# Host-turned x in six parts, and every third low half of layer 1 on GpSimd, in a four-layer fp32 forward pass

## The chip, the cores and the metric

The kernel runs on one NeuronCore of a Trainium2 chip. The metric is the device time of one execution in microseconds (us). Engines are called by the names of the profile: PE is the matmul engine (TensorE; PEld its weight loads), DVE is VectorE, ACT is ScalarE, POOL is GpSimd, SP is the engine that issues most DMAs.

## What is computed

x is 256 tokens by 2048 features. Four layers follow each other, each of the same outer form, and a last norm:

```python
proj = rmsnorm(x, norm_g) @ w_in          # 2048 -> 6160 .. 9224 columns
y = mixing(proj)                          # attention, mLSTM, RG-LRU, gated delta, ...
x = x + y @ w_out                         # 2048 -> 2048
...
def gated_delta_chunkwise(q, k, v, beta, g):      # layer 1
    a_mat = where(strict, (kbeta @ k^T) * gam, 0)
    t_inv = triangular_solve(eye + a_mat, eye)
    u, w = t_inv @ (v * beta), t_inv @ (kbeta * exp(decay))
    ...
```

Layer 0 is a chunked attention beside an mLSTM, layer 1 an RG-LRU beside the gated delta rule above, layers 2 and 3 are softmax attentions with rotary embedding. Everything is float32.

## The kernel before

**Products.** All big products are done in three passes of the fp32r type: a weight tile is split into a high half (its value rounded to fp32r) and a low half (weight minus high half), and so is the activation. Then high x high, high x low and low x high are added in PSUM. The weights stream from HBM in transfers of 1 MB into three buffers RAW. Each holds two **pieces** of 128 x 1024 values. For a piece ACT writes the high half (`split` of ACT, L981, WH<-RAW), DVE the low half (`split` of DVE, L1295, WL<-RAW,WH), in four buffers each, and PE does 24 products of 256 columns (L687 to L689) or 12 of 512 (L680 to L682). There are 626 pieces, numbered through the whole program. `load` on SP waits for the low halves of the transfer three before, which frees its buffer.

**Order.** Nothing is scheduled at run time but by semaphores: every engine runs through the pieces p = 0, 1, 2, ... in the same loop and does for each: the splits that fall due (`splits_of`, those of piece p+3 as a rule), the steps that the table `plan` puts half a place ahead of p, the `products` of p (PE), the `evacuate` of the job whose last piece p is (`ENDS`), and the steps that `plan` puts behind p. `put(slot, step, item, wants)` writes that table by hand, `begin_plan` for the start and `plan1` for layer 1. A step has the same place on every engine that takes part. If an engine waits within a step, all its later steps and splits wait behind it. Small products go through four PSUM banks PM in turn (`bank`): a step waits until the reader of the step four banks back is done.

**Start (layer 0).** x comes as rows of tokens. PE turns it to features by tokens with 32 transposes (`xt`, L703), ACT makes the high half of x times the norm's gain (L1048, XH<-PM), DVE the low half (L1349, XL). ACT also squares x for the norm (`squares`, L1056), DVE sums (`rms_a`), PE spreads the row scale (`rms_b`, L712). SP issues in this order: ident (64 KB of the constants), x part 0 of 4 (512 KB), both halves of weight transfer 0, x part 1, weight transfer 1, x parts 2 and 3, the rest of the constants (704 KB), row parameters (204 KB), weight transfer 2. POOL loads two bias tiles at once.

**Layer 1.** It starts at piece b1 = 177. Below, "piece 1.k" is piece b1+k. For two halves of four heads each it runs: `conv` (ACT scale L1142, DVE taps L1525, ACT silu L1148), `norm_sq` on POOL, `norm_sum`, `turn_v` (PE transposes L857 of v, ACT copies L1179), `diag` on POOL, `delta_a`, `delta_k`, `delta_q` (PE L864 to L877, ACT exponentials L1185 to L1187, DVE L1591 to L1611), `tri` in ten parts (a chain of small DVE operations, L1618 to L1643, and ACT copies L1194, L1199), `level_x` and `level_y` (PE L891, L905, L908, ACT L1209, DVE L1650, L1654), `solve1` to `solve4`, `onorm`, `gate_delta`, and `ty` (turned back for the product with w_out). Beside them run the eight blocks of the RG-LRU (`gate_lru`, `decay_lru`, `root_lru`, `scan`). POOL multiplies, from SBUF to SBUF: the evacuated conv inputs (L1794), the gates (L1800, L1874, L1881), and it clears and masks for `tri` (L1862 to L1864).

Of the kernel before, what the change touches and what calls it, by code (L numbers as in the profile page):

```python
# [20 lines left out]
LOOK = 3  # L21

# [118 lines left out]
def program(nc, I, out):  # L141
    ctx = ExitStack()
    with ctx:
# [167 lines left out]
        ENDS = {p: j for j, p in LAST.items()}  # L311
# [44 lines left out]

        def begin_plan():
# [65 lines left out]
        def plan1():  # L423
# [88 lines left out]

        def around(p):

            return ([x for s in (p - 0.5,) for x in plan.get(s, ())], plan.get(p, ()))


        s_c0, s_c1, s_mask, s_lam, s_tab, s_gw, s_fin, s_first, s_out = (
            sem(n) for n in ("s_c0", "s_c1", "s_mask", "s_lam", "s_tab", "s_gw", "s_fin", "s_first", "s_out"))
        s_x = [sem(f"s_x{i}") for i in range(4)]  # L520
        s_raw = [sem(f"s_raw{i}") for i in range(NRAW)]
        s_bias = [sem(f"s_bias{i}") for i in range(2)]
        s_hi, s_lo, s_mm, s_evA, s_evD = (sem(n) for n in ("s_hi", "s_lo", "s_mm", "s_evA", "s_evD"))
# [62 lines left out]
        n_id, n_cos, n_dil = COFF["ones"][0], COFF["cos"][0], COFF["dilated"][0]  # L586
# [5 lines left out]
        def sync(e):  # L592
# [8 lines left out]
            def load(n):  # L601
                j, k0, nk = raws[n]
                dst = RAW[n % NRAW][:, 0:nk * jobs[j].n].rearrange("p (k n) -> p k n", k=nk)
                if n >= NRAW:
                    e.wait_ge(s_lo, last_of_raw[n - NRAW] + 1)
                e.dma_start(dst, weights(n)).then_inc(s_raw[n % NRAW], 16)

            e.dma_start(C[:, 0:n_id], I["const"][:, 0:n_id]).then_inc(s_c0, 16)
            load_x(0)
# [3 lines left out]
            load_x(1)  # L613
            load(1)
            load_x(2)
            load_x(3)
            e.dma_start(C[:, n_id:n_dil], I["const"][:, n_id:n_dil]).then_inc(s_c1, 16)
            e.dma_start(RB[:, :], I["row"].partition_broadcast(128)).then_inc(s_c1, 16)
            load(2)
            again = pieces[F(2, "zs", 0)][0] + NRAW  # L620
            for n in range(NRAW, len(raws)):
                if n == again:
                    e.wait_ge(s_evD, at_D(2, "k1", 1))
                    e.dma_start(C[:, n_cos:n_dil], I["const"][:, n_cos:n_dil]).then_inc(s_tab, 16)
                load(n)
            o3 = out.rearrange("(t p) c -> p t c", p=128)
# [10 lines left out]
        def tensor(e):  # L637
# [8 lines left out]
            def products(p):  # L646
# [6 lines left out]
                e.wait_ge(s_lo, p + 1)  # L653
# [37 lines left out]

            def xt(i, b):
                layer, q = divmod(i, 8)
                if layer == 0:
                    e.wait_ge(s_x[q // 2], 16)
                    if q == 0:
                        e.wait_ge(s_c0, 32)
                else:
                    e.wait_ge(s_evD, at_D(layer - 1, "out", q // 2))
# [253 lines left out]
            steps = {"xt": xt, "rms_b": rms_b, "gates1": gates1, "gates2": gates2, "decay": decay, "mscores": mscores, "qkT": qkT,  # L953
# [19 lines left out]
        def scalar(e):  # L973
            e.dma_start(VC[:, :], I["vec"]).then_inc(s_c0, 16)
# [65 lines left out]

            def xt(i, b):
                layer, q = divmod(i, 8)
                if i == 0:
                    e.wait_ge(s_c0, 32)
                e.wait_ge(s_xt, i + 1)
# [216 lines left out]
            steps = {"xt": xt, "squares": squares, "root": root, "rms_a": rms_a, "gates1": gates1, "decay": decay, "pT": pT,  # L1262
# [11 lines left out]
            for p in range(NP):  # L1274
                before, after = around(p)
                for q in splits_of(p):
                    split(q)
                go(before)
                if p in ENDS:
                    evacuate(ENDS[p], p)  # L1280
# [10 lines left out]
        def vector(e):  # L1291
# [51 lines left out]

            def xt(i, b):
# [7 lines left out]
            def rms_a(layer, _):  # L1352
# [3 lines left out]
                e.reciprocal(rstd, rstd).then_inc(s_rstd)  # L1356
                if layer < 4:
# [377 lines left out]
            steps = {"xt": xt, "rms_a": rms_a, "rms_b": rms_b, "gates1": gates1, "gates2": gates2, "decay_row": decay_row,  # L1735
# [14 lines left out]
            for p in range(NP):  # L1750
                before, after = around(p)
                for q in splits_of(p):
                    split(q)
                go(before)
                if p in ENDS:
                    evacuate(ENDS[p], p)
# [14 lines left out]
        def gpsimd(e):  # L1771
            def evacuate(j, p):
# [41 lines left out]
            def norm_qk(_, b):  # L1814
                load_bias(0)
# [92 lines left out]
            for p in range(NP):  # L1908
                before, after = around(p)
                go(before)  # L1910
                if p in ENDS:
                    evacuate(ENDS[p], p)
# [6 lines left out]
def arrange(a):  # L1919
# [7 lines left out]
    m["x"] = _np.ascontiguousarray(a["x"][0])  # L1927
    t, c = _np.arange(128)[:, None], _np.arange(32)[None, :]
# [41 lines left out]
```

## Time and profile before

| | |
|---|---|
| median of 3 runs | 1970.77 us (1970.48 to 1971.33) |
| the profiled execution's own time | 1970.41 us |
| its span | 1968.6 us |
| PE busy | 1932.7 us (98%) |
| DVE busy | 1166.8 us (59%) |
| ACT busy | 1005.2 us (51%) |
| POOL busy | 172.6 us (9%) |
| HBM read | 334.47 MB, 171 GB/s over the span |

Busy is the time in which an engine executes instructions. PE's 98% leave 36 us in which it has no instruction. The chain that ended last is PE for 94% of the span. The granted clock of PE is full (2.4 GHz) in all but a few short stretches.

### The profile page before, as it was taken

Reading aid. Unit: us, or ns where it says so; the run is one execution under the profiler, and the core shown is the slowest. Engines: PE = TensorE matmul, PEld = TensorE weight load, DVE = VectorE, ACT = ScalarE, POOL = GpSimd, SP = SyncE. Lnnn points to the kernel's source line nnn. Section 1 sums busy time; section 2 is a strip of 40 time slices with the busy share of each in tenths; the row PEclk is TensorE's granted clock in tenths of the full one; section 3 lists DMA queues with packets and bytes.
Section 4 is the critical chain, followed back from the end, with each engine's and each line's share of the span. In section 5 each row is a group of like instructions: output and inputs, shape, how many; then the busy total and the mean of one; then the engine's idle time right before and its main releaser. Section 6 shows DMA issues by size and latency. Waiting matters only on the chain.

```text
span 1968.6 us, 28920 instructions
## 1 busy us (share of the span) xinstructions
PE 1932.7 (98%) x11932; PEld 1736.6 (88%) x11932; DVE 1166.8 (59%) x1635; ACT 1005.2 (51%) x1547; POOL 172.6 (9%) x162
## 2 busy tenths in 40 slices
PE   8999999999999999989999999999999999999997
PEld 7988888888899999889899899888889989988886
DVE  5445554555556776877566567655556656654554
ACT  5344445664556645755553344556554344445643
POOL 0000000110003211301001001000000101100110
PEclk9999999999999999999999999999999999999999
DMA  7555455555554443434555654554555554455553
GB/s 266 172 192 171 160 187 193 162 170 192 173 172 130 135 143 130 150 129 168 175 182 191 194 174 157 183 191 157 172 190 173 188 190 158 158 190 166 170 194 128
DMA packets 172851, 338.44 MB, mean 172 GB/s; under 512 B 9536, under 2 KB 9920, under 8 KB 172592
## 3 DMA queue, kind: packets, MB, share of 16 engines
q1 hardware_dynamic: 171632, 332.83, 51.4%
q0 software_dynamic: 944, 3.61, 0.6%
q8 instruction: 95, 1.56, 0.3%
q14 instruction: 36, 0.29, 0.0%
q10 hardware_dynamic: 144, 0.16, 0.0%
HBM read 334.47 MB, written 2.10 MB: 171 GB/s over the span
## 4 chain that ended last, share of the span: by engine, by line
PE 94%; DVE 3%; ACT 1%; issue 1%; DMA 0%; SPq 0%; DVEq 0%; ACTq 0%
PE ACC L680 17%; PE ACC L682 17%; PE ACC L681 17%; PE ACC L687 11%; PE ACC L688 11%; PE ACC L689 11%; DVE WL L1295 1%; DVE S L1525 1%; PE PM L770 1%; PE PM L703 1%; PE PM L785 1%; ACT WH L981 1%; PE PM L823 1%; PE PM L891 1%; PE PM L807 1%
## 5 line engine op out<-in xcount | busy, mean ns | idle before, releaser
L1295 DVE TENSOR_TENSOR WL<-RAW,WH 128x1024 fp32r<-128x1024 f32 x624 | 782.9, 1268 | 623.6 <-ACT WH L981 622.1
L981 ACT ACTIVATE WH<-RAW 128x1024 fp32r<-128x1024 f32 x626 | 652.2, 1054 | 544.8 <-PE ACC L682 303.3
L687 PE MATMUL ACC<-XH,WH 128*128 128x256 f32 x1920 | 554.2, 289 | 3.9 <-DVE WL L1295 3.7
L688 PE MATMUL ACC<-XL,WH 128*128 128x256 f32 x1920 | 545.9, 284 | 0.0
L689 PE MATMUL ACC<-XH,WL 128*128 128x256 f32 x1920 | 545.9, 284 | 0.0
L680 PE MATMUL ACC<-WH,XH 128*128 128x512 f32 x1024 | 406.5, 397 | 0.0
L682 PE MATMUL ACC<-WH,XL 128*128 128x512 f32 x1024 | 399.0, 390 | 0.0
L681 PE MATMUL ACC<-WL,XH 128*128 128x512 f32 x1024 | 398.7, 389 | 0.0
L687 PEld LDWEIGHTS ACC<-XH,WH 128*128 128x128 f32 x1920 | 371.5, 194 | 6.2 <-DVE WL L1295 4.7
L688 PEld LDWEIGHTS ACC<-XL,WH 128*128 128x128 f32 x1920 | 371.5, 193 | 0.9
L689 PEld LDWEIGHTS ACC<-XH,WL 128*128 128x128 f32 x1920 | 371.1, 193 | 0.0
L682 PEld LDWEIGHTS ACC<-WH,XL 128*128 128x128 f32 x1024 | 192.2, 188 | 40.6
L681 PEld LDWEIGHTS ACC<-WL,XH 128*128 128x128 f32 x1024 | 192.4, 188 | 39.0
L680 PEld LDWEIGHTS ACC<-WH,XH 128*128 128x128 f32 x1024 | 192.3, 188 | 38.8
L680 PE MATMUL ACC<-WH,YHB 128*128 128x512 f32 x256 | 100.8, 394 | 0.0
L680 PE MATMUL ACC<-WH,YHA 128*128 128x512 f32 x256 | 100.2, 391 | 0.0
L682 PE MATMUL ACC<-WH,YLB 128*128 128x512 f32 x256 | 99.8, 390 | 0.0
L682 PE MATMUL ACC<-WH,YLA 128*128 128x512 f32 x256 | 99.7, 389 | 0.0
L681 PE MATMUL ACC<-WL,YHB 128*128 128x512 f32 x256 | 99.6, 389 | 0.0
L681 PE MATMUL ACC<-WL,YHA 128*128 128x512 f32 x256 | 99.6, 389 | 0.0
L1806 POOL TENSOR_TENSOR S<-S 128x512 f32<-128x512 f32 x32 | 53.8, 1681 | 505.3 <-DVE S L1342 505.3
L682 PEld LDWEIGHTS ACC<-WH,YLB 128*128 128x128 f32 x256 | 48.0, 188 | 10.1
(328 smaller groups left out, 1646.2 us busy)
## 6 DMA issues: line engine op xcount, KB each, us to landing
RAW<-in_ev_w_in SPq DMA_DIRECT2D x71, 1024.0 KB, 4.9
RAW<-in_w_in_ab SPq DMA_DIRECT2D x64, 1024.0 KB, 5.2
RAW<-in_w_in_c SPq DMA_DIRECT2D x64, 1024.0 KB, 5.2
RAW<-in_od_w_in SPq DMA_DIRECT2D x48, 1024.0 KB, 5.0
RAW<-in_ev_w_out SPq DMA_DIRECT2D x16, 1024.0 KB, 4.9
RAW<-in_od_w_out SPq DMA_DIRECT2D x16, 1024.0 KB, 4.9
RAW<-in_w_out_ab SPq DMA_DIRECT2D x16, 1024.0 KB, 4.9
RAW<-in_w_out_c SPq DMA_DIRECT2D x16, 1024.0 KB, 4.9
```

The costliest lines, as they stand in the source:

```text
L680: e.matmul(o, th, hi[:, kk, :], start=f, stop=False)
L681: e.matmul(o, th, lo[:, kk, :], start=False, stop=False)
L682: m = e.matmul(o, tl, hi[:, kk, :], start=False, stop=l)
L687: e.matmul(o, wh, xh, start=f and g % 2 == 0, stop=False, skip_group_check=True)
L688: e.matmul(o, wh, xl, start=False, stop=False, skip_group_check=True)
L689: m = e.matmul(o, wl, xh, start=False, stop=l, skip_group_check=True)
L703: m = e.transpose(o[:, 256 * kk + 128 * t:256 * kk + 128 * t + 128], X3[:, t, 256 * q + 128 * kk:256 * q + 128 * kk + 128], ident)
L770: e.matmul(o[:, 128:384], qT[:, 128:256], kT, start=True, stop=True).then_inc(s_sc)
L785: m = e.transpose(o[:, c:c + 128], src[:, c:c + 128], ident)
L981: e.activation(hi, src, ACT.Copy).then_inc(s_hi)
L1295: e.tensor_tensor(lo, src, hi.bitcast(F32), ALU.subtract).then_inc(s_lo)
L1806: e.tensor_tensor(dst, dst, two(S6[:, 512 * i:512 * i + 512]), ALU.add).then_inc(s_rot)
```

## The change

**Start.** The host also hands over xT, x turned to features by tokens. SP loads it in six parts into Y, which is free then; ACT and DVE make XH and XL from there (`x0`), ahead of the split of the same features' weights. The transposes of layer 0 are gone. x itself, which the squares and the residual need, and the constants are loaded behind weight transfers 3 to 8. The squares stand at pieces 8 to 11 instead of 0 to 3, `rms_a` at 12, `rms_b` at 13.5, and the evacuation of job 0 seven pieces later. Ahead of piece 0 DVE clears 512 columns, PE does five products with them, and ACT one copy. The bias tiles wait until the row scale is there.

**Low halves.** 20 of the low halves of layer 1 (`BY_G`: pieces 1.35, 38, 41, 44, 52, 55, 58, 61, 64, 67, 70, 78, 81, 84, 87, 90, 93, 96, 99 and 102) are made by POOL. They count on a semaphore of their own, and PE and SP wait for whichever engine made the piece's low half (`low_of`).

**Later steps.** `turn_v` moves from 1.28 and 1.29 to 1.31 and 1.33 in half 0, and from 1.52 and 1.53 to 1.57 and 1.59 in half 1; the gates of half 0 by 3 to 4 places; levels, solves and gates of half 1 by 2.

```diff
+WARM = 5
...
-        ENDS = {p: j for j, p in LAST.items()}
+        ENDS = {p: (j,) for j, p in LAST.items()}
+        ENDS[LAST[0] + 7] = ENDS.pop(LAST[0])
...
+        X_PARTS = ((0, 2), (2, 2), (4, 2), (6, 2), (8, 4), (12, 4))
...
         def begin_plan():
-            for q in range(8):
-                put((-1, -0.5, 0.5, 2.5)[q // 2], "xt", q, 1)
+            put(-1, "warm")
             for b in range(4):
-                put((-0.5, 0.5, 2.5, 4)[b], "squares", b)
-            put(5, "rms_a", 0)
-            put(6.5, "rms_b", 0, 1)
+                put(8 + b, "squares", b)
+            put(12, "rms_a", 0)
+            put(13.5, "rms_b", 0, 1)
...
-            for half, at in ((0, (19, 22, 28, 29)), (1, (44, 48, 52, 53))):
+            for half, at in ((0, (19, 22, 31, 33)), (1, (44, 48, 57, 59))):
...
-                     (56, 58, 60, 61, 62), (82, 83, 85)),
-                    (1, (62, 63), (64, 66, 68, 69, 70), tuple(range(71, 81)), (81, 82, 84, 85, 86, 87), (89, 91, 93, 95, 96),
-                     (98, 99, 101))):
+                     (56, 58, 60, 61, 62), (85, 87, 89)),
+                    (1, (62, 63), (64, 66, 68, 69, 70), tuple(range(71, 81)), (83, 84, 86, 87, 88, 89), (91, 93, 95, 97, 98),
+                     (100, 101, 103))):
...
+        BY_G = [FIRST[J_OF[1, "qd", 0]] + i for i in (35, 38, 41, 44, 52, 55, 58, 61, 64, 67, 70, 78, 81, 84, 87, 90, 93, 96, 99, 102)]
+
+        def low_of(p):
+
+            g = sum(q <= p for q in BY_G)
+            return (s_loG, g) if p in BY_G else (s_lo, p + 1 - g)
...
+            load_xT(0)
             first = RAW[0][:, :].rearrange("p (k n) -> p k n", k=4)
             e.dma_start(first[:, 0:2, :], weights(0)[:, 0:2, :]).then_inc(s_first, 16)
             e.dma_start(first[:, 2:4, :], weights(0)[:, 2:4, :]).then_inc(s_raw[0], 16)
-            load_x(1)
+            load_xT(1)
             load(1)
-            load_x(2)
-            load_x(3)
-            e.dma_start(C[:, n_id:n_dil], I["const"][:, n_id:n_dil]).then_inc(s_c1, 16)
-            e.dma_start(RB[:, :], I["row"].partition_broadcast(128)).then_inc(s_c1, 16)
+            load_xT(2)
+            load_xT(3)
             load(2)
+            load_xT(4)
+            load_xT(5)
...
+            def warm(_, b):
+
+                e.wait_ge(s_warm, 1)
+                for _ in range(WARM):
+                    e.matmul(PM[0][:, :], S5[:, 1024:1152], S5[:, 1024:1536], start=True, stop=True)
...
+            def x0(q):
+                if q == 0:
+                    e.wait_ge(s_vec, 16)
+                for i, (k, n) in enumerate(X_PARTS):
+                    if k == 2 * q:
+                        e.wait_ge(s_xT[i], 16)
+                for n in (2 * q, 2 * q + 1):
+                    e.activation(XH3[:, n, :], Y[:, 256 * n:256 * n + 256], ACT.Copy, scale=gains[0][:, n:n + 1]).then_inc(s_xh)
...
         def gpsimd(e):
+            def split(p):
+                src, hi, lo = split_parts(p)
+                e.wait_ge(s_hi, p + 1)
+                e.tensor_tensor(lo, src, hi.bitcast(F32), ALU.subtract).then_inc(s_loG)
```

**How it moves instructions.** At the start of ACT's program (L1048 makes XH from PSUM, L981 a high half, L1056 squares) stands before:

```order
L1048 ACTIVATE XH<-PM,VC 128x256 x4
L981 ACTIVATE WH<-RAW 128x1024 x2
L1048 ACTIVATE XH<-PM,VC 128x256 x4
L1056 ACTIVATE SC,SM<-X 128x512 x2
L981 ACTIVATE WH<-RAW 128x1024 x3
```

and with the change (L1077 makes XH from Y, L1006 a high half):

```order
L1068 ACT_TABLE_LOAD
L1068 ACTIVATE SM<-S 128x1
L1077 ACTIVATE XH<-Y,VC 128x256 x2
L1006 ACTIVATE WH<-RAW 128x1024
L1077 ACTIVATE XH<-Y,VC 128x256 x2
```

The first high half stands behind two XH instead of four, and no square stands ahead of the third.

On ACT around pieces 1.28 to 1.31 (L1179 copies turned v, L1185 to L1187 are `delta_a`, L981 high halves) stands before:

```order
L1148 ACTIVATE S<-S 128x256 x2
L981 ACTIVATE WH<-RAW 128x1024
L1179 ACTIVATE S<-PM,SM 128x128 x4
L1185 ACT_TABLE_LOAD
L1185 ACTIVATE SC<-PM,SM 128x128
```

and with the change (the same three are L1215, L1221 to L1223 and L1006):

```order
L1184 ACTIVATE S<-S 128x256 x2
L1006 ACTIVATE WH<-RAW 128x1024
L1221 ACT_TABLE_LOAD
L1221 ACTIVATE SC<-PM,SM 128x128
L1222 ACTIVATE SC<-SC,SM 128x128
L1223 ACTIVATE SC<-SC,SM 128x128
L1006 ACTIVATE WH<-RAW 128x1024 x2
```

The copies of v are gone from between the silu of the conv and the exponentials of the second head.

On POOL from the second `diag` to the evacuation of job kd 1 stands before (L1794 multiplies conv inputs, L1862 to L1864 belong to `tri`):

```order
L1794 TENSOR_TENSOR S<-S,C 128x512 x2
L1862 MEMSET SC 128x1024
L1863 MEMSET SC 128x1024
L1864 TENSOR_TENSOR S<-SC,C 128x1024
L1794 TENSOR_TENSOR S<-S,C 128x512 x2
```

and with the change (L1825 is a low half, L1849 the multiply, L1918 to L1920 `tri`):

```order
L1825 TENSOR_TENSOR WL<-RAW,WH 128x1024
L1849 TENSOR_TENSOR S<-S,C 128x512 x2
L1825 TENSOR_TENSOR WL<-RAW,WH 128x1024
L1918 MEMSET SC 128x1024
L1919 MEMSET SC 128x1024
L1920 TENSOR_TENSOR S<-SC,C 128x1024
L1825 TENSOR_TENSOR WL<-RAW,WH 128x1024
L1849 TENSOR_TENSOR S<-S,C 128x512 x2
L1825 TENSOR_TENSOR WL<-RAW,WH 128x1024
```

The low halves of pieces 1.35, 1.38, 1.41 and 1.44 stand each ahead of the POOL work of the same place.

## Rows read from the trace of the kernel before

**Rows 1.** The page: busy us, share and instructions of each engine.
```profile
PE 1932.7 (98%) x11932; PEld 1736.6 (88%) x11932; DVE 1166.8 (59%) x1635; ACT 1005.2 (51%) x1547; POOL 172.6 (9%) x162
```

**Rows 2.** Waits of PE: waiting line, releaser, us in total, times, longest us.
```profile
PE PM L703 <- DMA X<-in_x: 8.8, 2, 6.1
PE PM L891 <- issue: 5.1, 1, 5.1
PE PM L864 <- ACT S L1179: 4.3, 1, 4.3
PE ACC L687 <- DVE WL L1295: 3.7, 3, 1.9
PE PM L905 <- DVE YLB L1513: 1.3, 1, 1.3
PE PM L905 <- ACT S L1179: 0.7, 1, 0.7
```

**Rows 3.** Timeline, 0 to 17 us: start, us, engine, line, operation, count [idle before].
```profile
6.13 1.97 PE L703 MATMUL PM<-C,X 128*128 128x128 f32 x8 [6.13 <-DMA X<-in_x]
...
10.07 2.02 ACT L981 ACTIVATE WH<-RAW 128x1024 fp32r<-128x1024 f32 x2
...
11.18 2.36 DVE L1295 TENSOR_TENSOR WL<-RAW,WH 128x1024 fp32r<-128x1024 f32 x2
...
12.46 0.58 PE L687 MATMUL ACC<-XH,WH 128*128 128x256 f32 x1
...
13.27 0.41 PE L687 MATMUL ACC<-XH,WH 128*128 128x256 f32 x1
...
15.09 0.28 PE L687 MATMUL ACC<-XH,WH 128*128 128x256 f32 x1
...
16.17 1.03 PE L703 MATMUL PM<-C,X 128*128 128x128 f32 x8
```

**Rows 4.** DMAs issued at 1.19, 1.66 and 8.61 us: size, us to landing.
```profile
X<-in_x SPq DMA_DIRECT2D x1, 512.0 KB, 4.9
RAW<-in_ev_w_in SPq DMA_DIRECT2D x1, 512.0 KB, 6.3
...
RAW<-in_ev_w_in SPq DMA_DIRECT2D x1, 1024.0 KB, 12.9
```

**Rows 5.** ACT's timeline ahead of piece 1.29.
```profile
640.11 0.81 ACT L1148 ACTIVATE S<-S 128x256 f32<-128x256 f32 x2 [1.16 <-DVE S L1525]
...
641.77 1.12 ACT L1179 ACTIVATE S<-PM,SM 128x128 f32<-128x128 f32 x4
```

**Rows 6.** Stretches: length, busy (count) of PE, PEld, DVE, ACT, POOL, granted clock, DMA.
```profile
643.00:645.00 2.00, 2.00 (x9) 1.82 (x8) 1.94 (x8) 1.22 (x2) 0.00 (x0) 0.50 0.03 8
...
848.00:854.00 6.00, 5.62 (x27) 5.65 (x28) 3.45 (x7) 5.76 (x10) 0.71 (x1) 0.52 0.00 1
```

**Rows 7.** Timeline of POOL and DVE where both read SBUF.
```profile
625.28 2.56 POOL L1794 TENSOR_TENSOR S<-S,C 128x512 f32<-128x512 f32 x2 [9.77 <-ACT S L1026]
...
626.61 2.31 DVE L1295 TENSOR_TENSOR WL<-RAW,WH 128x1024 fp32r<-128x1024 f32 x1 [2.70 <-ACT WH L981]
...
812.80 2.35 POOL L1864 TENSOR_TENSOR S<-SC,C 128x1024 f32<-128x1024 f32 x1
...
818.60 2.54 POOL L1800 TENSOR_TENSOR S<-S,RB 128x512 f32<-128x512 f32 x2 [1.81 <-ACT S L1032]
...
818.80 1.11 DVE L1630 TENSOR_TENSOR SC<-SC 128x16 f32<-128x16 f32 x1
819.94 1.22 DVE L1632 TENSOR_TENSOR SC<-SC 128x16 f32<-128x16 f32 x1
```

**Rows 8.** DVE's low half of piece 1.45.
```profile
697.11 1.22 DVE L1295 TENSOR_TENSOR WL<-RAW,WH 128x1024 fp32r<-128x1024 f32 x1 [1.43 <-ACT WH L981]
```

**Rows 9.** ACT's last copy of `tri`, half 1, and its high half of piece 1.84.
```profile
846.57 1.71 ACT L1199 ACTIVATE SC<-SC 32x256 f32<-32x256 f32 x4
...
850.84 1.04 ACT L981 ACTIVATE WH<-RAW 128x1024 fp32r<-128x1024 f32 x1
```

More of the change, by code:

```diff
@@ L585, in program @@
         x_rows = I["x"].rearrange("(t p) c -> p t c", p=128)
-        n_id, n_cos, n_dil = COFF["ones"][0], COFF["cos"][0], COFF["dilated"][0]
+        n_cos, n_dil = COFF["cos"][0], COFF["dilated"][0]
         block = ctx.enter_context(nc.Block())
@@ L604, in load, with load_xT @@
                 if n >= NRAW:
-                    e.wait_ge(s_lo, last_of_raw[n - NRAW] + 1)
+                    for p in range(last_of_raw[n - NRAW - 1] + 1 if n > NRAW else 0, last_of_raw[n - NRAW] + 1):
+                        e.wait_ge(*low_of(p))
                 e.dma_start(dst, weights(n)).then_inc(s_raw[n % NRAW], 16)
-            e.dma_start(C[:, 0:n_id], I["const"][:, 0:n_id]).then_inc(s_c0, 16)
-            load_x(0)
+            def load_xT(i):
+                e.dma_start(Y[:, part_of_x(i)], I["xT"][:, part_of_x(i)]).then_inc(s_xT[i], 16)
+            load_xT(0)
             first = RAW[0][:, :].rearrange("p (k n) -> p k n", k=4)
@@ L625, in sync @@
                 load(n)
+                if n < 7:
+                    load_x(n - 3)
+                if n == 7:
+                    e.dma_start(C[:, 0:n_dil], I["const"][:, 0:n_dil]).then_inc(s_con, 16)
+                if n == 8:
+                    e.dma_start(RB[:, :], I["row"].partition_broadcast(128)).then_inc(s_con, 16)
             o3 = out.rearrange("(t p) c -> p t c", p=128)
@@ L690, in products @@
                 m.then_inc(s_mm)
+            def warm(_, b):
+                e.wait_ge(s_warm, 1)
+                for _ in range(WARM):
+                    e.matmul(PM[0][:, :], S5[:, 1024:1152], S5[:, 1024:1536], start=True, stop=True)
             def xt(i, b):
                 layer, q = divmod(i, 8)
[L694 to L699, printed above, removed]
+                e.wait_ge(s_evD, at_D(layer - 1, "out", q // 2))
                 o = bank(b)
@@ L1039, in evacuate, with warm @@
                                      accum_out=ssq[:, 4 * t + J.b:4 * t + J.b + 1]).then_inc(s_sq)
+            def warm(_, b):
+                e.wait_ge(s_warm, 1)
+                e.activation(unused, S5[:, 1024:1025], ACT.Copy)
+            def x0(q):
[6 more added lines that the diff above has]
+                    e.activation(XH3[:, n, :], Y[:, 256 * n:256 * n + 256], ACT.Copy, scale=gains[0][:, n:n + 1]).then_inc(s_xh)
             def xt(i, b):
                 layer, q = divmod(i, 8)
[L1043 to L1045 removed]
+                e.wait_ge(s_xt, i - 7)
                 for kk in range(2):
@@ L1260, in subln @@
                     e.activation(ss, ss, ACT.Sqrt, bias=vec("eps"), scale=1.0 / 256).then_inc(s_sln)
-            steps = {"xt": xt, "squares": squares, "root": root, "rms_a": rms_a, "gates1": gates1, "decay": decay, "pT": pT,
+            steps = {"warm": warm, "xt": xt, "squares": squares, "root": root, "rms_a": rms_a, "gates1": gates1, "decay": decay, "pT": pT,
                      "norm_qk": norm_qk, "qkT": qkT, "scores": scores, "mix1": mix1, "pv": pv, "ty": ty, "conv": conv, "decays1": decays1,
@@ L1276, in scalar @@
                 for q in splits_of(p):
+                    if q < 8:
+                        x0(q)
                     split(q)
                 go(before)
-                if p in ENDS:
-                    evacuate(ENDS[p], p)
+                for j in ENDS.get(p, ()):
+                    evacuate(j, LAST[j])
                 go(after)
@@ L1342, in evacuate, with warm, x0 @@
                             e.tensor_tensor(t2[x], ps[y], sin[y], ALU.mult).then_inc(s_evD)
+            def warm(_, b):
+                e.memset(S5[:, 1024:1536], 0.0).then_inc(s_warm)
+            def x0(q):
+                e.wait_ge(s_xh, 2 * q + 2)
+                for n in (2 * q, 2 * q + 1):
+                    e.scalar_tensor_tensor(XL3[:, n, :], Y[:, 256 * n:256 * n + 256], gains[0][:, n:n + 1],
+                                           XH3[:, n, :].bitcast(F32), ALU.mult, ALU.subtract).then_inc(s_xl)
             def xt(i, b):
@@ L1356, in rms_a @@
                 e.reciprocal(rstd, rstd).then_inc(s_rstd)
+                if layer == 0:
+                    e.wait_ge(s_con, 32)
                 if layer < 4:
@@ L1733, in subln @@
                         e.scalar_tensor_tensor(y, y, ss[:, t, h:h + 1], row("subln"), ALU.mult, ALU.mult).then_inc(s_sub)
-            steps = {"xt": xt, "rms_a": rms_a, "rms_b": rms_b, "gates1": gates1, "gates2": gates2, "decay_row": decay_row,
+            steps = {"warm": warm, "xt": xt, "rms_a": rms_a, "rms_b": rms_b, "gates1": gates1, "gates2": gates2, "decay_row": decay_row,
                      "decay": decay, "mscores": mscores, "norm_qk": norm_qk, "scale_k": scale_k, "scores": scores, "mix1": mix1,
@@ L1752, in vector @@
                 for q in splits_of(p):
-                    split(q)
+                    if q < 8:
+                        x0(q)
+                    if q not in BY_G:
+                        split(q)
                 go(before)
-                if p in ENDS:
-                    evacuate(ENDS[p], p)
+                for j in ENDS.get(p, ()):
+                    evacuate(j, LAST[j])
                 go(after)
@@ L1909, in gpsimd @@
                 before, after = around(p)
+                for q in splits_of(p):
+                    if q in BY_G:
+                        split(q)
                 go(before)
-                if p in ENDS:
-                    evacuate(ENDS[p], p)
+                for j in ENDS.get(p, ()):
+                    evacuate(j, LAST[j])
                 go(after)
```

21 lines of the change are left out of this document (11 added, 10 removed).

## Prediction

> **What bounds the kernel now.** First the busy times: PE has instructions for 1932.7 of 1968.6 us [rows 1], so it is the bound, and a change can gain three things: the 36 us in which PE has nothing, the time in which its clock is halved, and work taken off PE. No other engine is busy for over 60% of the span. Next the waits of PE, which say who ends its idle time [rows 2]: 8.8 us for x at the start, and in layer 1 5.1 us at `level_x`, 4.3 us at `delta_a` for ACT's copies of v, 3.7 us in three waits for DVE's low halves, and 1.3 and 0.7 us at `level_y`. All of it lies where the change works. Then the timelines at these places, for what stood ahead of the releaser on its engine, and the stretches, for the clock: after the 4.3 us wait PE runs at 1.2 GHz from 642.4 to 645.7 (0.50 in the row), after the 5.1 us wait up to 853.8 (0.52) [rows 6]. At half clock each us costs half a us: 1.6 and 2.7 us. The 3.7 us of low halves hold two waits of 1.9 us at pieces 1.45 and 1.47, and behind the second the clock is halved for 3.4 us, another 1.7.
>
> **Start, term by term.** (a) *First product.* It starts at 12.46 us, 2.4 us behind the start of the first high half at 10.07 [rows 3]. The weights for that one had landed at 1.66 + 6.3 = 7.96 [rows 4]; ACT was busy with four XH. From there to the landing of weight transfer 2 at 8.61 + 12.9 = 21.5 the queue brought 5004 KB (all that SP issued in between), 369 KB per us. In the new order 320 KB less stand ahead of the first weights (256 KB of xT for 64 KB of constants and 512 KB of x) and one bias tile of 128 KB less beside them: 1.2 us, so 6.8 us, and the two XH are done by then, since their 256 KB come first. 6.8 + 2.4 = 9.2: **-3.3 us**. Bounds: 0 (if nothing lands earlier) and -4.5. (b) *Transposes.* Of 32, 16 stand behind the first product, in two groups of 1.03 us [rows 3]: **-2.1**. (c) *Pace.* The first 8 products follow each other in 0.21 us, later ones in 0.12 (0.41 and 0.28 us long in the rows) [rows 3]: PE had been idle but for two short groups of transposes. The five products of zeros keep it busy from about 1.5 us. Their cost is nothing as long as they end before 9.2. No row shows a float32 product of 512 columns; by the transposes, 8 in 1.97 us at the low pace, one column takes 1.9 ns, two passes of 512 columns 2 us, five products 10 us, at the high pace 5. They begin slow and turn fast on the way, so 7 to 8 us, done in time; at worst they hold the first product to 11.5. **-0.7**, between -0.8 and +2.3. (d) *New waits.* Piece 2 needs the third part of xT, at 369 KB per us 12.4 us, then two XH, a high half and a low half of about 3.1 us: 15.5, against 15.0 at which PE is through with piece 1. Later pieces have over 1 us in hand. **+0.5**, between 0 and 3. The squares, `rms_a` and the late loads of x and the constants lie beside products and cost nothing: they come 5 us ahead of the step that needs them; without that cover they would delay the evacuation of job 0, for which two pieces are left. Sum of the start: **-5.6 us**.
>
> **Turns (1.28 to 1.34).** ACT copied v at 641.77, behind a silu that waited for DVE's taps until 640.11 [rows 5], and PE's `delta_a` waited for the bank. With the turns three and four places later the second `delta_a` finds a bank that is long free: 4.3 + 1.6 = -5.9. What is late next: DVE and ACT come no sooner through this stretch than before, since their conv steps don't move, so PE now meets them at 1.31, where the bank of `turn_v` 1 waits for DVE's reading of `delta_k` 1. From the spacing of these steps I get 1.1 us; bounds 0 and 4.3. **-4.8**. In half 1 the wait of 0.7 goes [rows 2]: **-0.7**.
>
> **Low halves on POOL.** DVE saves 1.2 us for each (two in 2.36) [rows 3]. POOL has no row of this instruction. Its nearest is a multiply of the same size, 2.35 us [rows 7]. POOL has the time: it needs the high half, ready some 7 us before PE needs the low one. But the two engines block each other. A low half of DVE that began at 626.61, under a POOL multiply that lasted until 627.84, took 2.31 us instead of 1.23, and of `tri` two operations of 0.2 us took 1.11 and 1.22 us under POOL's two at 818.60 [rows 7]. So a low half on POOL holds DVE's next operation with two SBUF inputs for up to 2.35 us and saves it 1.2: up to 1.2 us lost wherever DVE has no pause, and that is where PE waits for it, from 680 to 705. There stand 1.41 and 1.44: +2.4 at most. Against that, 1.35 and 1.38 free DVE earlier, and there it pauses anyway. I take **+0.8** at piece 1.45, whose low half came at 697.11 [rows 8], and leave both waits of 1.9 us as they are; bounds -5.1 (both waits and the slow clock gone) and +2.4. The Trainium skill states this blocking as a rule, in "SBUF — State Buffer", section "Who interferes with whom": a VectorE instruction with two SBUF inputs and a GpSimd instruction that reads SBUF take one port pair, and whichever comes second waits for the whole of the other. The trace agrees (2.31 against 1.23 us); without the rule the sum would be 5.9 us lower, the first rival below. The other 15 low halves lie where pieces come 5 us or more behind them, but for 1.78, 1.81 and 1.84.
>
> **Levels of half 1 (1.81 to 1.89).** `level_x` waited for ACT's last copy of `tri`, begun at 846.57 [rows 9]. Two places later PE does pieces 1.82 and 1.83 in that time, until 849.0, and goes straight on: -5.1, -2.7 for the clock, and -1.3 for the `level_y` that stood behind the turned gates, which now come later. But piece 1.84 comes forward too. Its high half begins at 850.84 on an ACT that has no pause from 840 on [rows 9], and ends at 851.9. DVE needed 1.2 us from there; POOL needs 2.35 and so ends at 854.3. PE is there after `level_x` (3.76 us at half clock, 1.9 at full) at 850.9: **a new wait of 3.5 us**, at most the old 5.1. Whether it halves the clock is open (waits of 1.9 us did it once and once not): +0.8, half of 3 us at half clock, weighed by one half. -9.1 + 3.5 + 0.8 = **-4.8**. The gates and solves that move behind it end well ahead of the last pieces of `out`, which need them.
>
> **Sum.** -5.6 - 4.8 - 0.7 + 0.8 - 4.8 = -15.1 us. The profiled execution took 1970.41 us, 0.36 less than the median of the runs, 1970.77. So 1955.3 by its time, and **1955.7 us** by the median.
>
> **Rivals.** *POOL helps in full* (chance 0.19): the blocked operations fall into DVE's pauses, the waits at 1.45 and 1.47 go with their slow clock, and the 0.8 as well: 5.9 us lower, 1949.8. For it: DVE no longer waits for the high halves of 1.41 and 1.44. Against it: its chain in 680 to 705 has hardly a pause. *Waits moved, not removed* (0.17): at 1.84 PE waits as long as it did at `level_x`, clock included (ACT is the bound there), or POOL delivers 1.78 or 1.81 late: +4.8, 1960.5. For it: ACT's unbroken row of work. *The start gives half* (0.12): the first product comes no earlier, since the products of zeros or the weights hold it: +3.3, 1959.0. *Slower* (0.05): POOL's low halves hold DVE so often that DVE becomes the bound from 1.35 to 1.102. Each costs DVE 1.2 us net; all 20 on the path are +24, against -15.9 of the other terms (the sum without its 0.8), so +8.1: 1978.9. It decides from 14 low halves on the path on. Against it: DVE has pauses (59% busy over the span [rows 1]), and outside `tri` it waits for PE or ACT before most low halves. That the change doesn't do what it says is no case of its own: the orders above show it.
>
> **How the numbers follow.** The forecast has 0.47. The range: the first rival with the 1.1 us of the turns and 1 us more at the start is 1947.7; the two middle ones together 1963.8. I give 1947 to 1964, which leaves 0.05 for the slower case and the rest for sizes off by more. A measurement of this kernel can tell about 0.2% (3.9 us) from no change. Faster by more than that: all cases but the slower one, less something for several bad bounds at once, 0.89; within it 0.06; slower 0.05.
>
> **What would show it.** The first product at 9 to 9.5 us, then 0.12 us apart at once, and piece 8 some 6.6 us sooner than before. PE's wait at `delta_a` gone, a shorter one at `turn_v`. POOL's low halves at 2.35 to 2.6 us, with DVE operations of over 1 us under them. Waits at 1.45 and 1.47 still there. The 5.1 us gone from `level_x`, and a wait of 3 to 4 us at the first product of 1.84, put down to POOL. It is wrong if POOL's low half takes 3 us or more, if PE waits at 1.78 or 1.81, or if the first product comes later than 10.5.

## The result, and the profile after

| | before | after |
|---|---|---|
| median of the runs, us | 1970.62 (1970.40 to 1971.33, 4 runs) | 1960.99 (1959.75 to 1961.94, 4 runs) |
| ratio to before | 1 | 0.995, interval 0.9933 to 0.9967 |
| the profiled execution, its span, us | 1970.41, 1968.6 | 1961.8, 1960.0 |
| low halves by DVE, by POOL | 626, 0 | 606, 20 |

The change is faster by 9.6 us by the medians of the runs (8.6 by the two spans). I had predicted a gain of 15.1 us and a time of 1955.7 us. The busy times first, as in [rows 1]:

```profile
PE 1932.9 (99%) x11910; PEld 1732.5 (88%) x11910; DVE 1169.2 (60%) x1616; ACT 1005.9 (51%) x1548; POOL 220.1 (11%) x182
```

PE is busy for as long as before, though the 32 transposes of x are gone (five products of zeros stand in their place): its gain is the idle time. POOL has 47.5 us more. DVE has lost 20 low halves at 1.2 us each, and yet is busy for 2.4 us more: 24 us of work left it and 26 came back. That is the first sign of what follows. The waits of PE (engine, line, what it waited for: us in total, times, longest), as in [rows 2]:

```profile
PE ACC L713 <- DVE WL L1333: 8.2, 6, 3.9
PE ACC L713 <- POOL WL L1825: 2.9, 1, 2.9
PE PM L901 <- DVE S L1652: 1.5, 2, 1.3
PE PM L722 <- DVE S L1383: 1.5, 1, 1.5
PE PM L882 <- DVE S L1652: 1.4, 1, 1.4
PE PM L930 <- DVE YLB L1560: 0.5, 1, 0.5
```

L713 is the first product of a piece, L1333 DVE's low half, L1825 POOL's, L882 `turn_v`, L901 `delta_k`. The 8.8 us for x, the 5.1 at `level_x` and the 4.3 at `delta_a` are gone; waits for low halves grew from 3.7 us to 11.1. (The 3.7 us before were 1.6 us at piece 1.45, 1.9 at 1.47 and 0.3 at 1.39; my prediction took the first for 1.9 too.) The start, as in [rows 3], from the timeline of the changed kernel (start, us, engine, line, operation, count, idle before it):

```profile
1.46 6.87 PE L722 MATMUL PM<-S 128*128 128x512 f32 x10 [1.46 <-DVE S L1383]
...
5.88 1.06 ACT L1006 ACTIVATE WH<-RAW 128x1024 fp32r<-128x1024 f32 x1 [0.19 <-DMA RAW<-in_ev_w_in]
...
6.97 1.23 DVE L1333 TENSOR_TENSOR WL<-RAW,WH 128x1024 fp32r<-128x1024 f32 x1 [0.36 <-ACT WH L1006]
...
8.25 0.39 PE L713 MATMUL ACC<-XH,WH 128*128 128x256 f32 x1
8.47 0.28 PE L714 MATMUL ACC<-XL,WH 128*128 128x256 f32 x1
8.59 0.27 PE L715 MATMUL ACC<-XH,WL 128*128 128x256 f32 x1
```

The weights landed at 5.9 us, where I had 6.8, and the rest of the chain is the predicted 2.4 us: first product at 8.25. The products of zeros end as it starts, and the pace is 0.12 us from the second product on.

One term of the start isn't in my sum. The step `rms_b` (L712 before, L737 now) stands before at piece 6, where PE waited 0.58 us for it and came 1.2 us late out of pieces 6 and 7. At its new place, piece 13.5, it costs 0.4 us and has no wait:

```profile
35.92 0.67 PE L712 MATMUL PM<-C 128*128 128x256 f32 x2 [0.58 <-issue]
```

```profile
49.41 0.60 PE L737 MATMUL PM<-C 128*128 128x256 f32 x2
```

To see where time came and went I counted the products off in order and took for each piece its start after minus its start before:

| stretch | predicted | measured |
|---|---|---|
| start, up to piece 1.22 | -5.6 | -6.8 |
| 1.23 to 1.28 | 0 | +0.1 |
| turns, 1.29 to 1.38 | -4.8 | -4.3 |
| 1.39 to 1.50 | +0.8 | **+5.1** |
| 1.51 to 1.61 | -0.7 | -0.9 |
| 1.62 to 1.81 | 0 | +1.1 |
| levels, from 1.82 on | -4.8 | -2.9 |
| sum | -15.1 | -8.6 (-8.7 by the rounded rows) |

From piece 1.105 to the end the distance stays at 8.6 us. So one stretch holds most of the miss, and it is the one where I had expected POOL's low halves to do little. The timeline of DVE and POOL there, in the changed kernel:

```profile
672.08 2.69 POOL L1825 TENSOR_TENSOR WL<-RAW,WH 128x1024 fp32r<-128x1024 f32 x1 [5.41 <-ACT WH L1006]
...
672.43 0.18 DVE L1675 STREAM_SHUFFLE SC<-SC 128x8 f32<-128x8 f32 x1
672.65 2.15 DVE L1677 TENSOR_TENSOR SC<-SC 128x8 f32<-128x8 f32 x1
674.84 0.17 DVE L1679 TENSOR_TENSOR SC<-SC 128x8 f32<-128x8 f32 x1
...
678.96 2.34 POOL L1825 TENSOR_TENSOR WL<-RAW,WH 128x1024 fp32r<-128x1024 f32 x1
...
678.97 3.41 DVE L1333 TENSOR_TENSOR WL<-RAW,WH 128x1024 fp32r<-128x1024 f32 x1
```

Read it by pairs. Under POOL's low half of 1.41 a shuffle of DVE, with one input, keeps its 0.18 us; the next operation, with two inputs from SBUF, takes 2.15 us where its twin takes 0.17. The second low half is that of 1.44: DVE's own low half of 1.42 begins 0.01 us behind it and takes 3.41 us instead of 1.22. (In between two more `tri` operations take 1.2 us each under POOL's conv multiplies, L1849; in the kernel without low halves on POOL two of them take 1.0 and 1.2 us as well.) And PE stands at 1.42:

```profile
682.43 0.58 PE L713 MATMUL ACC<-XH,WH 128*128 128x256 f32 x1 [3.87 <-DVE WL L1333]
```

PE's granted clock is halved in most of the 4 us around and after that, and again after the 2.9 us wait at 1.84 (length, busy of PE, PEld, DVE, ACT, POOL with counts, granted clock, DMA share, GB/s):

```profile
849.00:853.00 4.00, 4.00 (x23) 4.00 (x23) 4.00 (x3) 0.93 (x1) 2.99 (x1) 0.57 0.83 260
682.00:686.00 4.00, 3.57 (x19) 3.57 (x20) 3.67 (x17) 0.00 (x0) 0.00 (x0) 0.58 0.59 182
```

### The profile page after: what moved, and what is told of

Its sections match the earlier page's. It is cut to its first block, busy times and chain, and to the rows that moved or that the text cites. A ratio compares the mean times of both kernels' runs of the same rounds, so it can differ in the third digit from the quotient of the medians.

```text
span 1960.0 us, 29183 instructions
## 1 busy us (share of the span) xinstructions
PE 1932.9 (99%) x11910; PEld 1732.5 (88%) x11910; DVE 1169.2 (60%) x1616; ACT 1005.9 (51%) x1548; POOL 220.1 (11%) x182
## 4 chain that ended last, share of the span: by engine, by line
PE 90%; DVE 5%; ACT 3%; issue 1%; DMA 0%; POOL 0%; SPq 0%; DVEq 0%; ACTq 0%
PE ACC L706 17%; PE ACC L708 17%; PE ACC L707 17%; PE ACC L713 11%; PE ACC L714 11%; PE ACC L715 11%; DVE WL L1333 2%; DVE S L1572 1%; ACT WH L1006 1%; PE PM L795 1%; DVE SC L1677 1%; PE PM L810 1%; PE PM L848 1%; PE PM L832 1%; PE PM L833 1%
## 5 line engine op out<-in xcount | busy, mean ns | idle before, releaser
L1333 DVE TENSOR_TENSOR WL<-RAW,WH 128x1024 fp32r<-128x1024 f32 x604 | 763.1, 1277 | 603.8 <-ACT WH L1006 602.1
L1006 ACT ACTIVATE WH<-RAW 128x1024 fp32r<-128x1024 f32 x626 | 652.1, 1054 | 530.3 <-PE ACC L708 301.2
L713 PE MATMUL ACC<-XH,WH 128*128 128x256 f32 x1920 | 553.7, 288 | 11.1 <-DVE WL L1333 8.2
L713 PEld LDWEIGHTS ACC<-XH,WH 128*128 128x128 f32 x1920 | 370.8, 193 | 14.9 <-DVE WL L1333 10.4
L1825 POOL TENSOR_TENSOR WL<-RAW,WH 128x1024 fp32r<-128x1024 f32 x20 | 49.3, 2467 | 117.0 <-ACT WH L1006 117.0
```

The lines of the kernel that those rows point to most:

```text
L713: e.matmul(o, wh, xh, start=f and g % 2 == 0, stop=False, skip_group_check=True)
L1006: e.activation(hi, src, ACT.Copy).then_inc(s_hi)
L1333: e.tensor_tensor(lo, src, hi.bitcast(F32), ALU.subtract).then_inc(s_lo)
L1825: e.tensor_tensor(lo, src, hi.bitcast(F32), ALU.subtract).then_inc(s_loG)
```

## Experiments

Theory: a low half on POOL holds DVE's next operation with two SBUF inputs for most of its 2.3 to 3.0 us and saves DVE 1.2 us, so the 20 low halves cost time, and the rest of the change is worth what I gave it. Rival: they relieve DVE, and the loss at 1.42 comes from PE arriving 11 us sooner at a DVE that can't.

### Four corners: start, moves, low halves

The start alone, the start with the low halves, the start with the later steps (the moves), and all three: that shows whether a part costs or gives something only beside another.

Start alone (turns, levels, solves and gates back at their places, every low half on DVE):

```diff
-            for half, at in ((0, (19, 22, 31, 33)), (1, (44, 48, 57, 59))):
+            for half, at in ((0, (19, 22, 28, 29)), (1, (44, 48, 52, 53))):
...
-        BY_G = [FIRST[J_OF[1, "qd", 0]] + i for i in (35, 38, 41, 44, 52, ...)]
+        BY_G = []
```

> The start alone, with the turns, levels, solves and gates at their old places and every low half on DVE. In the changed kernel piece 15 began 6.8 us sooner than before. Theory: this gain reaches the end whole, about 1963.8 us (ratio 0.9965). Rival: layer 1 gives part of it back, since its ACT and DVE work is paced by itself there and PE only waits longer: 1965 to 1967 us.

Measured: 1963.6 us (1963.4 to 1964.51), ratio 0.9962 (0.995 to 0.9975). The start reaches the end whole, 6.8 us.

The whole change with every low half on DVE (`BY_G = []` alone):

> The whole change, but all low halves on DVE. Theory (a low half on POOL holds DVE's operations with two SBUF inputs for longer than it saves it): the 3.9 us wait at piece 1.42 falls to about 2.2, the 1.3 us wait for the delta bank at 1.70 goes, the 2.9 us wait at 1.84 falls to about 1.7: some 4 us less, 1957 us. Rival (POOL's low halves do relieve DVE, and the wait at 1.42 comes from PE arriving 11 us sooner): DVE pays 1.2 us more for each of 1.38, 1.41 and 1.44 on its path, and the wait grows: 1963 to 1965 us.

Measured: **1954.09 us** (1953.45 to 1955.91), ratio 0.9915 (0.9902 to 0.9929). The low halves on POOL cost the change 6 to 7 us; without them it beats both kernels. By the pieces they cost 5.7 us; the other 2.0 us between these two profiled executions lie ahead of the first low half on POOL (0.3 at the start, and a slow stretch behind 1.22 that is longer in the changed kernel). PE's waits without them:

```profile
PE ACC L713 <- DVE WL L1333: 9.8, 6, 2.9
PE PM L722 <- DVE S L1383: 1.5, 1, 1.5
PE PM L882 <- DVE S L1652: 1.4, 1, 1.4
PE PM L930 <- DVE YLB L1560: 0.5, 1, 0.5
PE PM L901 <- DVE S L1652: 0.4, 2, 0.2
```

The wait at 1.42 is not shorter but gone, since DVE's low halves through this stretch take 1.22 us again; the one at `delta_k` went from 1.3 to 0.2. The sum for low halves is 9.8 us all the same: 2.9 at 1.39, 1.6 and 1.9 at 1.45 and 1.47, 0.8 at 1.48, 2.3 at 1.84, and 0.4 at piece 0.

Low halves at the old places (start and POOL's 20, without the moves):

> The start and POOL's 20 low halves, with turns, levels, solves and gates at their old places: beside the run of the start alone this is what the low halves do by themselves. Theory (they hold DVE): 1 to 4 us above the start alone, 1965 to 1968 us. Rival (relief: the waits of 1.9 us at 1.45 and 1.47 go with their slow clock, and nothing new comes): 1958 to 1961 us.

Measured: 1966.41 us (1965.87 to 1969.6, 11 runs), 2.8 above the start alone. So POOL's low halves cost time in either arrangement, more where the moves bring PE up sooner. The rival's reason for the wait at 1.42 falls with the corners together: with low halves on POOL it is 3.9 us at the old places too, where PE comes 7.7 us sooner than before; without them there is none, though PE comes 10.4 us sooner.

### Which of the twenty

The four under `tri` of half 0 (1.35, 1.38, 1.41, 1.44) back on DVE:

> The whole change, but the low halves of pieces 1.35, 1.38, 1.41 and 1.44 on DVE, the other 16 still on POOL. Theory: only the wait at 1.42 shrinks, by 1.7 to 2 us: about 1959 us. Rival (relief): 1963 to 1965 us. Third: the harm is at the other places (1.67 to 1.84), then this equals the changed kernel, 1961, and the run without any low half on POOL has the whole difference.

Measured: 1958.8 us (1957.43 to 1959.7), 4.7 above none. They are worth about 1.5 us of the piece table (at 1.54 its pieces lie within 0.1 us of the run with none). The rest of the difference stands at 1.70, where this kernel falls 1.1 us behind the one with none, and from 1.82 on, 3.0 us. The first of these is the same hold, by POOL's low half of 1.70, on the taps of a convolution (in the changed kernel; six taps take 2.45 us elsewhere):

```profile
787.95 2.37 POOL L1825 TENSOR_TENSOR WL<-RAW,WH 128x1024 fp32r<-128x1024 f32 x1 [9.41 <-ACT WH L1006]
...
788.88 3.69 DVE L1572 SCALAR_TENSOR_TENSOR S<-S,VC 128x255 f32<-128x255 f32 x6 [2.95 <-ACT S L1180]
```

DVE comes 1.2 us late out of the taps, so late to the bank of `delta_k`, and PE waits 1.3 us where it had waited 0.2.

Only those of 1.78, 1.81 and 1.84 on POOL:

> All low halves on DVE but those of pieces 1.78, 1.81 and 1.84. Theory: the three are the 3.0 us that the trace shows lost between 1.81 and 1.85 (PE waits 2.9 us at 1.84 for POOL, which needs 2.35 us from the high half where DVE needs 1.2, and at half clock after it): 1957.1 us. Rival: that loss belongs to the low halves before or behind (1.67, 1.70 and 1.87 and later): 1954 to 1955 us.

Measured: 1956.1 us (1956.02 to 1957.65); from 1.81 to 1.85 its pieces fall 2.7 us behind the run with none. The theory stands, but the wait itself is the smaller part of it. With DVE's low half PE waits 2.3 us at 1.84 too; with POOL's it waits 2.9, and 0.3 at 1.82. The rest is the clock, halved for 3.4 us behind it (1.7 us). That happened in all four profiled executions that have the moves and POOL's low half of 1.84, and in two of the six with DVE's, so part of the 1.7 us is chance.

The eleven that I took for harmless:

> Low halves on POOL at 1.52, 1.55, 1.58, 1.61, 1.64 and from 1.87 on (11 of 20), the other nine on DVE. Theory: they hold DVE as often as the others, but where pieces lie 5 us or more behind DVE: the same as without any, 1954.1 us within 0.7. Rival: each costs PE something (7 us over 20 is 0.35 each): 1958 us.

Measured: 1957.16 us (1954.8 to 1959.32), 3 above none, with runs so far apart that the times alone settle nothing. The profiled execution, the slowest of the five, has new waits and a slow stretch around 1.89, worth 2.9 us. POOL's low half of 1.90 lies over a scan of DVE:

```profile
859.96 2.43 POOL L1825 TENSOR_TENSOR WL<-RAW,WH 128x1024 fp32r<-128x1024 f32 x1 [9.27 <-ACT WH L1006]
860.18 2.76 DVE L1747 TENSOR_TENSOR_SCAN Y<-S 128x256 f32<-128x256 f32 x1
```

The scan takes 0.69 us elsewhere. It stands on DVE ahead of the subtractions of the levels (L1697, L1701), whose results the next `level_x` on PE needs: 1.1 us in two waits, none with all on DVE, and 3.4 us at half clock. So "harmless" was wrong for those from 1.87 on. In the change itself this doesn't show (from 1.88 to 1.90 it goes as the kernel with none). PE had already lost more at 1.84 there, so one hold probably covered the next; no run shows that by itself.

### Hold or lateness

An idle subtract on POOL at the 20 places, all low halves on DVE (`DUM` is a scratch tile of its own):

```diff
-                e.tensor_tensor(lo, src, hi.bitcast(F32), ALU.subtract).then_inc(s_loG)
+                e.wait_ge(s_dum, next(dum))
+                e.tensor_tensor(DUM[:, :], DUM[:, :], DUM[:, :], ALU.subtract).then_inc(s_dum)
```

> The whole change with all low halves on DVE (1954.1 us), and at the 20 places of the change POOL does an idle subtract of 128x1024 within a scratch tile of its own: the hold without the relief. Theory (POOL's reading of SBUF holds DVE's operations with two SBUF inputs): DVE pays the hold and gets no low half taken off, so at least as slow as the change, 1961 to 1966 us; only at 1.84, where PE waited for POOL itself, it is 1.2 us better. Rival (the change loses because POOL's low half itself is late, or by its waits, not by a hold of DVE): 1954 to 1956 us.

Measured: **1969.64 us** (1967.57 to 1969.95, 11 runs), 15.5 above the kernel without it, though nothing waits for its result. PE's waits in it are all for DVE; the three largest:

```profile
PE ACC L715 <- DVE WL L1335: 10.4, 7, 3.5
PE PM L918 <- DVE SC L1703: 4.1, 2, 3.5
PE PM L903 <- DVE S L1654: 2.1, 2, 1.8
```

(L918 is `level_x`, L903 `delta_k`.) PE never waits for POOL here, so it is the hold. Lateness of POOL itself shows in the change at one place alone, 1.84, where PE waits 2.90 us for POOL, against 2.3 for DVE in the kernel with none (1.15 here, where PE comes later). I had given 1961 to 1966 us; the holds add up to more once DVE has all the low halves too.

The same with three memsets of the tile in place of the subtract:

```diff
+                for _ in range(3):
+                    e.wait_ge(s_dum, next(dum))
+                    e.memset(DUM[:, :], 0.0).then_inc(s_dum)
```

> As the run with the idle subtract, but at each place POOL fills the scratch tile three times with zeros (0.95 us each in the trace), which reads nothing. Theory (it is the reading side that is shared): DVE's subtracts keep their 1.22 us under it and the time is that without POOL's low halves, 1954.1 us. Rival (any access of POOL to SBUF slows DVE): 1957 us or more.

Measured: 1954.37 us (1952.8 to 1954.91), ratio 0.9919 (0.9905 to 0.9932), as without any. POOL works longer (57 us in 60 memsets, 50 in 20 subtracts) and holds nobody. Its other work isn't what matters either: ACT waits 3.1 us for POOL's gates in both of these kernels. DVE's operations under the memsets:

```profile
676.74 2.97 POOL L1828 MEMSET DUM<- 128x1024 f32 x3
```

```profile
677.16 0.21 DVE L1679 TENSOR_TENSOR SC<-SC 128x48 f32<-128x48 f32 x1
677.40 0.21 DVE L1681 TENSOR_TENSOR SC<-SC 128x48 f32<-128x48 f32 x1
677.53 1.22 DVE L1335 TENSOR_TENSOR WL<-RAW,WH 128x1024 fp32r<-128x1024 f32 x1
```

So it is POOL's reading of SBUF that holds DVE, and above all DVE's operations with two SBUF inputs that are held. The Trainium skill says this in "SBUF — State Buffer", section "Who interferes with whom": an operation of VectorE with at most one SBUF input doesn't contend, outside its two-port modes, and one with two does with a GpSimd instruction that reads, not with one that only writes. The traces agree: 0.18 us for the shuffle, 1.22 under the memset, 3.41 under the subtract.

One input alone doesn't make an operation safe. A plain copy of DVE under POOL's gate multiply in the changed kernel, and the same copy with POOL idle:

```profile
810.36 0.77 DVE L1670 COPY SC<-VC 128x128 f32<-128x128 f32 x1
```

```profile
671.15 0.22 DVE L1670 COPY SC<-VC 128x128 f32<-128x128 f32 x1
```

### Start and turns

The change without low halves on POOL, and without the products of zeros (`WARM = 0`):

> As the whole change without low halves on POOL (1954.1 us), and without the five products of zeros. Theory: the first product still starts at 8.2 us, since it waits for DVE's low half, but the first products follow each other at half the clock for some 2 to 4 us, which loses half of that: 1.0 to 2.0 us more, 1955.5 us. Rival: the products of zeros, which end within 0.4 us of the first product, buy nothing: the same 1954 us, and the pace is 0.12 us from the first.

Measured: 1956.06 us (1954.55 to 1957.32), against 1954.09; the runs overlap, the trace doesn't leave it open. The first product is at 8.33, and the pace:

```profile
9.11 0.41 PE L713 MATMUL ACC<-XH,WH 128*128 128x256 f32 x1
9.32 0.41 PE L714 MATMUL ACC<-XL,WH 128*128 128x256 f32 x1
...
12.22 0.29 PE L713 MATMUL ACC<-XH,WH 128*128 128x256 f32 x1
12.35 0.28 PE L714 MATMUL ACC<-XL,WH 128*128 128x256 f32 x1
```

It is 0.21 us up to 12.1 and 0.12 behind. From piece 4 on this kernel is 1.3 us later than the one with the products of zeros, 0.2 of it in the first product. So they are worth 1.1 to 1.3 us, and the first product isn't later for them. My 0.7 was priced against the kernel before, whose transposes had already brought the pace to 0.12 after eight products.

The change without low halves on POOL, with the turns at their old places:

> As the whole change without low halves on POOL (1954.1 us), but the turns at their old places (28, 29 and 52, 53): the share of the turns alone. Theory from the two traces (piece 1.50 gains 3.1 us by them, piece 1.61 another 0.9): 4.0 us slower, 1958.1 us. My prediction gave the turns 5.5 us: 1959.6 us. Rival: the waits of 2.9 us at 1.39 and 1.4 us at 1.31, which the later turns bring, take nearly all: 1 to 2 us slower, 1955.5 us.

Measured: 1960.99 us (1958.91 to 1961.39), 6.9 above. By the pieces, without the 1.4 us that its slow stretch behind 1.22 adds, the turns are worth 5.7 us at 1.38, 3.1 at 1.50, and 4.0 at 1.61. So half 0 gives 3.1 and half 1 0.9. The other 1.5 us of its trace is a clock stretch at 1.85. What takes 2.6 of the 5.7 back stands at 1.39, on ACT and DVE (trace of the changed kernel):

```profile
666.98 0.42 ACT L1184 ACTIVATE S<-S 128x256 f32<-128x256 f32 x1 [2.16 <-DVE S L1572]
667.30 1.04 ACT L1006 ACTIVATE WH<-RAW 128x1024 fp32r<-128x1024 f32 x1
```

```profile
669.66 0.39 PE L713 MATMUL ACC<-XH,WH 128*128 128x256 f32 x1 [2.10 <-DVE WL L1333]
```

The high half (L1006) stands behind a silu (L1184), which waits for DVE's taps. That gave the next run, with these edits of the plan (the silu become a step of their own): in layer 1 the two silu of a convolution step one piece later on ACT, behind one more high half; all low halves on DVE.

```diff
                 put(L(1, *CONV[c]) + 3, "conv", (c, 1))
+                if c < 6:
+                    put(L(1, *CONV[c]) + 2, "silu", (c, 0))
+                    put(L(1, *CONV[c]) + 4, "silu", (c, 1))
```

> The whole change without low halves on POOL (1954.1 us), and in layer 1 ACT's two silu of each convolution step one piece later than its scaled copies, behind one more high half. Theory: the waits of PE at 1.39, 1.45 and 1.47 are DVE's low halves behind high halves that stood behind a silu (DVE waits 1.43 us for ACT at each); these 1.4 us go three times: about 1950 us. Rival: DVE's taps hold the low half as long as ACT holds the high one, or the silu now delays v, k and q and the waits turn up at the delta steps: 1954 us or more.

Measured: **1945.14 us** (1944.18 to 1945.87), ratio 0.9873 (0.986 to 0.9887), the fastest of all. Its waits of PE, whole but for sums under 0.5:

```profile
PE ACC L716 <- DVE WL L1338: 2.3, 1, 2.3
PE PM L725 <- DVE S L1388: 1.5, 1, 1.5
PE PM L933 <- DVE YLB L1565: 0.5, 1, 0.5
```

Not three times 1.4 us but every wait from 1.31 to 1.48 is gone, 8.5 us of them in the kernel without this step; by the pieces it gains 10.1 us between 1.28 and 1.50, of which a slow stretch behind 1.22 hides 1.6 in this execution. DVE had waited for the high half, the high half for the silu, the silu for DVE's taps: a ring in which each wait fed the next one.

### The change once more

> The changed kernel once more, beside the three below on one chip. The stretches at half clock behind the column sums of the norms (pieces 1.22 and 1.48) last 3.4 or 6.8 us in executions of one and the same code, and each 3.4 us cost 1.7: so 1960 to 1962 us, and the waits at 1.39, 1.42 and 1.84 as before. If the profiled execution has the short stretch at 1.22, its pieces from 1.23 on lie 1.7 to 1.9 us sooner than in the first profile.

Measured: 1960.0 us (1957.26 to 1962.32), ratio 0.9948 (0.9935 to 0.9962). The expectation of 1960 to 1962 holds, and so do the waits at 1.39 (2.1 us) and 1.84 (2.9). But there is no wait at 1.42; one of 1.5 us stands at 1.43 instead. DVE had done the low half of 1.42 at its 1.22 us, at 676.78. POOL's low half of 1.44 begins at 680.37, when a `tri` operation is next on DVE; that one takes 2.07 us, and the low half of 1.43 comes behind it. Which operation is held depends on who begins first, and in the first profile that was a matter of 0.01 us (678.96 and 678.97); one or another is held in both. From 1.39 to 1.47 this execution lost 0.7 us less than the first, so the cost of these low halves itself differs between executions of one code. Its stretch behind 1.22 was a long one, so the other part of the expectation wasn't tried by it.

## Why the prediction was right and wrong

The time, 1961, lies in the range and is faster by more than 0.2%, as I gave 0.89 for. The number 1955.7 was 5.3 us too low.

- **Start, -5.6, measured -6.8.** (a) was -4.2 instead of -3.3: the first weights landed 2.1 us sooner, where the rate of the queue gave 1.2. Of the 2.1 us 0.5 is that SP issues them that much earlier (1.19 for 1.66 us), which I left out. (b), (c) and (d) went as forecast and are a little worse in sum: read from the starts of the products, the transposes -1.7 (a group pushes the next product back by 0.8 to 0.9 us, not by the 1.03 that its row is long), the pace -0.8, new waits in pieces 0 to 2 +0.8, so -1.7 for -2.3. The rest is `rms_b`, which I had put at nothing: -1.2 at pieces 6 and 7, +0.4 at its new place, so -0.8. So the mechanisms of (a) to (d) were right; what the term left out is the earlier issue and a step that I hadn't priced.
- **Turns, -4.8, measured -4.3 and then +2.6.** The new wait at `turn_v` is there as predicted, 1.4 us for 1.1. What failed in this term is "what is late next": I looked one stop ahead, to 1.31, and stopped. The gain of 4 us that is left arrives at 1.39 as earliness against ACT, whose high half stands behind a silu. Half 1, -0.7, measured -0.9.
- **Low halves, +0.8, shown 5.7 by the pieces, 6 to 7 by the medians.** This is the step that failed. I had the hold and its price from [rows 7], about 1.2 us net, and had the right two places, 1.41 and 1.44. But I took their cost as 0.8 and counted the rest as free but for 1.84, whose later end from POOL (1.15 us) and slow clock (0.8) stand in the term of the levels: 2.8 us in all. (The rest are 16, not 15 as I wrote.) The traces show holds of 1.2 to 2.2 us, and they count at 1.42 and 1.43 (1.5 net by 1.50), at 1.70 (1.1) and from 1.78 on (about 3, the wait for POOL at 1.84 and the clock behind it among them); a further one at 1.89 was covered. That is beyond my bound of +2.4. Distance between the moved piece and PE didn't protect: what was held was a step of layer 1's own chain (taps, scan, `tri`) whose result PE needs soon.
- **The rivals.** POOL helps in full is refuted by the run without low halves on POOL. Waits moved, not removed gave 1960.5, within 0.5 us of the measured time, and that is luck: its two conditions, a wait at 1.84 as long as the old one with its clock or POOL late for 1.78 or 1.81, didn't come. (For 1.81 POOL was done 0.1 us before PE needed it.) The slower case went by the right mechanism, with far fewer than 14 on the path.
- **Levels, -4.8, measured -2.9.** The new wait at 1.84 for POOL was 2.9 us for 3.5, and the clock was halved behind it, 1.7 us where I had weighed 0.8. From 1.81 to 1.85 that makes -3.4; 0.5 more goes by 1.105. Without POOL there the levels give 6.0.
- **Left out:** +0.95 us between 1.47 and 1.50, in the start alone too. In the kernel before PE ran at half clock from 1.47 on and so met no wait at 1.48; now it runs at full clock there, waits 0.8 us, and the slow stretch comes with the column sums behind it. That is read from the two traces; no run was made for it.
- **What makes up the +5.1 of 1.39 to 1.50:** 2.6 given back by the turns, this 0.95, and 1.5 by the low halves.
- **Waits at 1.45 and 1.47 "stay":** in the changed kernel the first is gone and the second is 0.9 us, because PE had lost the time at 1.42 already; with all low halves on DVE they are there as before, 1.6 and 1.9.
- **The rest of the change** is worth 16.3 us by the medians (1954.1 against 1970.4), and my terms without the 0.8 came to 15.9. The nearness is partly luck: the turns gave back 2.6 us, and the start and the levels gave more than I had put down.

## What to carry to other kernels

Moving an elementwise operation to GpSimd relieves VectorE only as far as GpSimd doesn't read SBUF while VectorE works on two SBUF inputs. Where it does, compare the hold (here 1.2 to 2.2 us) with the saving (here 1.2 us), for each place and for what is held, not for the piece that was moved. When a wait is removed, follow the gain from stop to stop until it is spent: here it met a high half behind a silu, and moving that silu by one piece was worth 9 us, nearly as much as the whole change. And a part of a change may cost what another part brings: run the parts alone and together.

## What the runs showed of the hardware

The granted clock falls in the column sums of the norms, although the rows show PE busy throughout: they are 16 products of one column, 32 instructions in the rows, in 5.4 us (from 605.12 us on in the changed kernel, where the clock falls at 606.9). Executions of the same code differ in how long it stays down. The changed kernel and the kernel with all low halves on DVE, from 604 to 616 us:

```profile
604.00:616.00 12.00, 12.00 (x79) 12.00 (x79) 6.80 (x23) 5.25 (x7) 1.48 (x4) 0.72 0.40 117
```

```profile
604.00:616.00 12.00, 12.00 (x93) 12.00 (x92) 7.69 (x22) 5.13 (x8) 1.48 (x4) 0.86 0.54 176
```

The first is 6.8 us at half clock (1.2 of 2.4 GHz), the second 3.4 with 14 products more in the 12 us. Each 3.4 us costs 1.7 us, and with two to five slow stretches in layer 1, these and those behind waits, a kernel's own runs lie up to 5 us apart (1957.3 to 1962.3 for the changed kernel). What decides between the two lengths stays open. A difference under 2 us was therefore read from the pieces of the traces, with the slow stretches taken out.
